# A hybrid encoder layer on one core: weight halves copied ahead of mixed sums, identity turns between phases, and two late waits

## The reference, cut to what matters

```python
xn = rms_norm(h, g_attn_pre)
qa, ka, va, qb, kb, vb = split(xn @ w_in)
ya = mixer_a(...)        # 8 query heads, 2 key heads, softmax over all 2048 keys
yb = mixer_b(...)        # 8 heads, three dilated windows with a bias table
y = concat([rms_norm(ya, g_out_a), rms_norm(yb, g_out_b)]) @ w_out
h = h + rms_norm(y, g_attn_post)
f = square(relu(rms_norm(h, g_mlp_pre) @ w_ff1)) @ w_ff2
h = h + rms_norm(f, g_mlp_post)
h = h + sigmoid(rms_norm(h, g_ple) @ w_ple_gate) * (p @ w_ple_proj)
```

## Time and profile before

| | |
|---|---|
| three runs | 3360.53, 3360.77, 3361.61 us |
| profiled execution | 3360.36 us, span 3358.6 us |
| PE busy | 3294.1 us (98%) |
| DVE, ACT, POOL busy | 2278.8 (68%), 1853.5 (55%), 1851.7 us (55%) |
| mean granted PE clock | 0.996 |

### The profile page before, as it was taken

The page is one execution under the profiler, slowest core; times in us unless marked ns, Lnnn a source line. Parts: engine busy times, 40 slices in busy tenths (PEclk is TensorE's granted clock), DMA queues, the critical chain, the costliest instruction groups (busy, mean ns, idle before and its releaser), DMA issues.

```text
span 3358.6 us, 48304 instructions
## 1 busy us (share of the span) xinstructions
PE 3294.1 (98%) x17246; PEld 2767.0 (82%) x17246; DVE 2278.8 (68%) x4080; ACT 1853.5 (55%) x3576; POOL 1851.7 (55%) x1434
## 2 busy tenths in 40 slices
PE   8999999999999989998999999999999999999999
PEld 7888878888888879997888888888888888888887
DVE  6556579999999989997646565555746556565555
ACT  3221178888888879998434354344543435443333
POOL 5555534454452168883477732777407776057771
PEclk9999999999999999999999999999999999999999
DMA  5554433444442234344244456444474444744444
GB/s 192 165 185 152 142 104 139 154 169 157 157 143 75 62 88 104 95 99 173 78 138 151 151 194 251 144 154 147 163 250 163 147 155 144 262 155 143 143 149 158
DMA packets 223915, 503.39 MB, mean 150 GB/s; under 512 B 105428, under 2 KB 123420, under 8 KB 204476
## 3 DMA queue, kind: packets, MB, share of 16 engines
q1 hardware_dynamic: 214332, 486.57, 43.9%
q10 hardware_dynamic: 9344, 13.73, 1.1%
HBM read 417.09 MB, written 95.58 MB: 153 GB/s over the span
## 4 chain that ended last, share of the span: by engine, by line
PE 44%; DVE 4%; ACT 2%; POOL 2%; issue 1%; DMA 1%; SPq 0%; ACTq 0%; DVEq 0%
PE feed_bank L1906 41%; DVE feed_sums L2397 1%; PE feed_bank L1991 1%; PE feed_bank L1897 1%; POOL feed_v_hl L1863 1%; POOL feed_qT L1863 0%; PE feed_bank L2014 0%; DMA feed_y_in<-scr_yB 0%; DVE feed_xT L2321 0%; ACT feed_rl L2201 0%; ACT feed_rl L2203 0%; PE feed_bank L2046 0%; POOL feed_kT L1863 0%; ACT feed_v_hl L2186 0%; DVE feed_sums L2394 0%
## 5 line engine op out<-in xcount | busy, mean ns | idle before, releaser
L1863 POOL TENSOR_TENSOR feed_v_hl<-feed_w_raw,feed_v_hl 128x1024 fp32r<-128x1024 f32 x176 | 437.6, 2496 | 138.6 <-ACT feed_v_hl L2186 133.0
L1906 PE MATMUL feed_bank<-feed_v_hl,feed_comb 128*128 128x512 f32 x1776 | 416.5, 390 | 3.1 <-POOL feed_v_hl L1863 3.1
L1906 PEld LDWEIGHTS feed_bank<-feed_v_hl,feed_comb 128*128 128x128 f32 x1776 | 331.8, 188 | 74.5 <-POOL feed_v_hl L1863 6.3
L1126 DVE TENSOR_TENSOR mixa_pT<-mixa_turned,mixa_pT 128x512 fp32r<-128x512 f32 x512 | 350.9, 685 | 58.9 <-ACT mixa_pT L1068 52.5
L1068 ACT ACTIVATE mixa_pT<-mixa_turned 128x512 fp32r<-128x512 f32 x512 | 306.7, 599 | 118.7 <-PE mixa_turned L1004 99.6
L949 PE MATMUL mixa_out_acc<-mixa_pT,mixa_v_hl 128*128 128x512 f32 x1028 | 365.7, 437 | 0.2
L2413 DVE TENSOR_TENSOR feed_total<-feed_total,feed_bank 128x512 f32<-128x512 f32 x352 | 223.9, 682 | 190.2 <-PE feed_bank L1906 187.4
L2382 DVE TENSOR_TENSOR feed_comb<-feed_rl,feed_comb 128x256 fp32r<-128x256 f32 x128 | 138.9, 1085 | 312.1 <-ACT feed_comb L2205 311.7
L1906 PE MATMUL feed_bank<-feed_xT,feed_v_hl 128*128 128x512 f32 x1488 | 344.3, 390 | 3.1 <-ACT feed_rl L2201 3.1
L2201 ACT ACTIVATE feed_rl<-feed_bank 128x512 f32<-128x512 f32 x128 | 76.4, 597 | 490.2 <-PE feed_bank L1906 483.5
L1906 PEld LDWEIGHTS feed_bank<-feed_xT,feed_v_hl 128*128 128x128 f32 x1488 | 280.2, 188 | 62.0 <-issue 3.7
(11 more groups left out here) (263 smaller groups left out, 7099.6 us busy)
## 6 DMA issues: line engine op xcount, KB each, us to landing
feed_w_raw<-scr_wT SPq DMA_DIRECT2D x160, 512.0 KB, 3.3
feed_w_raw<-w_tail_dram SPq DMA_DIRECT2D x128, 512.0 KB, 3.5
proj_w_raw<-w_in_dram SPq DMA_DIRECT2D x36, 1024.0 KB, 5.3
feed_v_hl<-scr_wG SPq DMA_DIRECT2D x34, 1024.0 KB, 5.1
feed_w_raw<-w_ff_dram SPq DMA_DIRECT2D x64, 512.0 KB, 3.4
feed_qT<-scr_wG SPq DMA_DIRECT2D x17, 1024.0 KB, 4.8
feed_kT<-scr_wG SPq DMA_DIRECT2D x17, 1024.0 KB, 5.1
scr_table<-scr_bias SPq DMA_DIRECT2D x8, 1520.0 KB, 9.0
```

The costliest lines, as they stand in the source:

```text
L1126: ve.tensor_tensor(pT[1][:, s % NR, :], turned[s % 2][:], pT[0][:, s % NR, :].bitcast(F32), ALU.subtract).then_inc(lo_done, 1)
L1863: pool.tensor_tensor(w_sp[slot][:, 1, :], w_raw[:, slot, :], w_sp[slot][:, 0, :].bitcast(F32), ALU.subtract).then_inc(w_lo, 1)
L1906: mm = pe.matmul(dst, lhs, rhs, start=start, stop=stop)
```

## The change

Three things change.

1. ACT's list in the feed: at chunk (m, g, 0, 0) it takes two upper weight halves, `weight_hi(i + 3)` as before and `weight_hi(i + 4)`, and only then `mixed_hi(g, 3)`; at the next chunk it takes none.
2. PE turns the identity, with no reader, at five places: 14 times at the end of the projection, 36 times at the start of mixer B behind the four that are there, 16 times at the end of mixer B, 32 times at the start of the feed and 24 times behind the first turn of data there.
3. SP no longer waits for the last store of each row tile at the end of the projection: SP waits in mixer A in front of the load of mixer B's v, and ACT in front of its first turned tile. At the end of mixer B SP waits only for the stores of the first buffer; the last store is awaited in the feed behind the first raw weight loads. For that `st_out`, `y_st` and a semaphore `y_last` move to objects that outlive the phase.

```diff
@@ FeedInputs, FirstInputs
+        self.y_st = k.sb("y_st", [P, 2, 4, HD], side="right")
+        self.y_last = k.sem("y_last")
+        self.st_out = k.sems("st_out", TT)
@@ project_phase, SP and PE
             for s in st_out:
-                sp.wait_ge(s, 16 * (4 * NBLK + 1))
+                sp.wait_ge(s, 16 * (4 * NBLK))
+            for _ in range(14):
+                pe.transpose(tp[0][:, 0:P], ident[:], ident[:])
@@ mixer_a_phase, SP before heads.load_v, ACT before the loop over tiles
+            for s in first.st_out:
+                sp.wait_ge(s, 16 * (4 * NBLK + 1))
+            for s in first.st_out:
+                act.wait_ge(s, 16 * (4 * NBLK + 1))
@@ mixer_b_phase, SP and PE
-            for s in y_out:
-                sp.wait_ge(s, 32 * NHB + 16)
+            sp.wait_ge(y_out[0], 32 * NHB + 16)
+            for _ in range(36):
+                pe.transpose(score[1][:, BANK:BANK + P], ident[:], ident[:])
+            for _ in range(16):
+                pe.transpose(score[0][:, 0:P], ident[:], ident[:])
@@ feed_phase, SP behind the raw loads, PE, ACT
+            sp.wait_ge(feed.y_last, 32 * NHB + 16)
+            keep_on(32)
             turn(0, 0)
+            keep_on(24)
                 for i, c in enumerate(FF):
-                    if i + 3 < NFF and FF[i + 3][0] == "m":
+                    if i + 3 < NFF and FF[i + 3][0] == "m" and FF[i - 1][2:] != (0, 0):
                         weight_hi(i + 3)
...
                     elif c[2:] == (0, 0):
+                        weight_hi(i + 4)
                         mixed_hi(c[1], 3)
```

More of the change, by code:

```diff
@@ L260, in project_phase @@
         qo_ready, ko_ready = k.sem("qo_ready"), k.sem("ko_ready")
-        st_out = k.sems("st_out", TT)
+        st_out = first.st_out
         qo_out, ko_out = k.sem("qo_out"), k.sem("ko_out")
@@ L1174, in mixer_b_phase @@
         y_part = k.sb("y_part", [P, 2, 2, P])
-        y_st = k.sb("y_st", [P, 2, 4, HD])
+        y_st = feed.y_st
         score = [ctx.enter_context(nc.psum_tensor(f"mixb_score{i}", [P, 2 * BANK], F32)) for i in range(2)]
@@ L1189, in mixer_b_phase @@
         rden_done, y_ready = k.sem("rden_done"), k.sem("y_ready")
-        y_out = k.sems("y_out", 2)
+        y_out = [k.sem("y_out"), feed.y_last]
         K_DMAS, Q_DMAS, V_DMAS = heads.K_DMAS, heads.Q_DMAS, heads.V_DMAS
@@ L1995, in first_out, with keep_on @@
                 mm.then_inc(acc_done, 1)
+            def keep_on(count):
+                for _ in range(count):
+                    pe.transpose(acc[3][:, 0:P], ident[:], ident[:])
+            keep_on(32)
             turn(0, 0)
+            keep_on(24)
             for t in range(TT):
```

## The result

| | before | changed |
|---|---|---|
| median of 11 runs each | 3360.80 us | 3369.82 us |
| lowest and highest | 3359.00, 3364.43 | 3368.59, 3373.65 |
| profiled execution, its span | 3360.36, 3358.6 us | 3369.76, 3368.0 us |

The ratio is 1.0026, with a 95% interval of 1.0018 to 1.0034: 9.0 us slower. The forecast was 3371.4 us, on the slower side.

What follows compares the result with a forecast made beforehand. The prediction took PE, busy for 98% of the span, as the bound. Its terms, 16.4 - 1.65 - 1.0 - 3.2 = +10.6 us, gave 3371.4 us on the median, range 3347 to 3378.

Steps and rivals of the forecast that it cites:

- The boundary: Feed, chunk (m, g, 2, 0): POOL's subtraction delays DVE's fifth sum 2.34 us, PE starts 1.26 later, thirteen times: +16.4 us.
- no obstacle: Rival at the feed boundary: DVE's fifth sum passes ahead of or beside POOL's subtraction, 13 x 0.36 saved; 3350.2 us, chance 0.20.
- either way: Rival at the feed boundary: the order of DVE's sum and POOL's subtraction swaps at about half the places; 3360.8 us, chance 0.14.
- Projection to A: Projection to mixer A: without SP's store wait the phase starts at 433.7, not 435.32: -1.65 us; clock 1.00 anyway.
- A to B: Mixer A to mixer B: 36 turns hold the clock, DVE's first bias addition comes 1.0 earlier, POOL's row then gates: -1.0 us.
- B to feed: Mixer B to feed: earlier start without the store wait -1.3, first turn -0.25, first 12 products at full clock -1.65: -3.2 us.
- cold-turns rival: Phase changes: turns don't hold the clock and stand in front of needed work; with the port effect 3386 us, chance 0.08.

Runs made afterwards that it cites:

- Experiment 1: Kernel before with only ACT's new weight order (upper half for chunk (m, g, 2, 0) copied ahead of the mixed sums): 3376.71 us, ratio 1.0044.
- experiment 3: Changed kernel, but POOL waits ahead of the lower half of chunk (m, g, 2, 0) until DVE's fifth mixed sum is done: 3356.14 us, ratio 0.9984.
- experiment 4: Kernel of experiment 3, with DVE also adding the first product's tile 0 results ahead of the mixed lower half: 3345.69 us, ratio 0.9956.
- experiment 5: Kernel before with the late store waits alone, without turns and with ACT's old weight order: 3356.70 us, ratio 0.9986.
- experiment 6: Kernel before with the turns alone, without late store waits and with ACT's old weight order: 3357.58 us, ratio 0.9988.
- experiment 2: Changed kernel with ACT's old weight order, so turns and late store waits alone: 3355.29 us, ratio 0.9982.
- experiment 8: Changed kernel with DVE adding the first product's tile 0 results ahead of the mixed lower half, POOL not held: 3352.90 us, ratio 0.9974.
- experiment 7: Kernel of experiment 6 without the 16 turns ending mixer B and with 72 instead of 32 starting the feed: one run, 3364.58 us.

## Why the prediction was right

**The boundary: right in mechanism and size.** Forecast was a fifth sum that ends 2.34 later and a PE start 1.26 later, thirteen times, 16.4. Against the start of PE's twelve products the fifth sum now ends 2.20 later. Those products take 4.47 from start to start (2218.08 to 2222.55) for 3.25 before, 1.22 more; the sum of the trace is 15.6. The mean is 1.20 for 1.26. Experiment 1 shows that the order causes it, experiment 3 that of the order the overlap does. One reading was loose: of the five sums from 1660.2 to 1670.3 only the three beside a subtraction of POOL take 2.6 us; two take 1.25 beside POOL copies of 1.2. One sum per POOL operation holds. The port rivals (no obstacle, either way) are out: the wait of 1.6 stands at all 13 places. The Trainium skill, "SBUF — State Buffer", "Who interferes with whom", says that a DVE instruction with two SBUF inputs contends with a GpSimd instruction that reads SBUF, and that whichever issues first has the ports to itself to the end. The rows agree: 2.61 behind POOL, 0.41 ahead of it. The same section of the Trainium skill says that with one SBUF input there is no contention; DVE's additions, whose other input is a PSUM bank, take 0.64 each beside POOL's two subtractions in experiment 4.

**Projection to A: -2.04 for -1.65.** About 1.5 of it is the step; 0.5 is luck, since PE's last product ended at 431.31 in this execution and at 431.83 before, and nothing ahead of it was changed. Phase A's start came 0.45 behind PE's last turn. The 14 turns do stand in front: experiment 5 has none, and phase A starts 1.61 behind PE's last product there, 1.97 here. The step's other statement, that the clock is at 1.00 there anyway, rested on one execution: in experiment 1, where nothing in this phase was changed, the same 24 turns behind the same 3.48 us ran at 0.50.

**A to B: mis-sized, -0.26 for -1.0.** The clock held and the first bias addition came 0.74 sooner behind the phase's first turn, but PE's first turn of the probabilities then waited 1.34 for POOL, and by the last product of B 0.26 was left. That POOL's row gates PE was in the step; how much of the 1.0 it eats was not. Even the 0.26 isn't shown to be the turns' work: from B's first turn to its last product the three traces without turns take 381.03 to 381.98 us, the eight with them 380.54 to 381.70.

**B to feed: -3.12 for -3.2.** From B's last product to the second tile's turn: -1.31 by the wait, the rest by the clock. The two hang together: without the turns the wait's part was lost again (experiment 5, -0.05), the turns alone gave -1.84 (experiment 6), and where the clock fell as the 16 turns began both gave only -1.93 (experiment 2).

**The end: 0.7 unforeseen.** From the last boundary to the last products the changed kernel gained 10.09 - 9.40: a wait of PE for DVE's norm at 3294.07, 0.93 before, is 0.23 now. The same obstacle is at work. In the chain to that norm DVE subtracts two SBUF operands while POOL subtracts weights, and this row is 0.71 shorter, because it begins 0.90 us into POOL's instruction (3291.08) and no longer about 0.2:

```profile
3281.90 3.29 DVE L2447 TENSOR_TENSOR feed_comb<-feed_y_in,feed_comb 128x1024 fp32r<-128x1024 f32 x1 [1.04 <-ACT feed_comb L2225]
...
3291.98 2.58 DVE L2468 TENSOR_TENSOR feed_comb<-feed_y_in,feed_comb 128x1024 fp32r<-128x1024 f32 x1 [1.04 <-ACT feed_comb L2246]
```

In experiments 2, 3, 4 and 8 the row takes 3.31, 2.58, 2.67 and 3.20, and PE's wait is 0.95, 0.22, 0.32 and 0.84: always 2.35 or 2.36 less.

Sum of the profile: 15.6 - 2.04 - 0.09 - 0.26 - 3.12 - 0.7 = +9.4, as measured, where -0.09 is what phase A itself gained. The forecast sum was +10.6. The terms missed by -0.8, -0.5, +0.7, +0.1 and -0.7; that they cancel in part is luck. The cold-turns rival falls by the rows at 1.00 and by experiment 7; where turns did run at 1.2 GHz (experiment 2), it cost 1.2 us in the feed, and the clock was at 1.00 again before the first turn of data. In the rival "no obstacle" the price was too small: its 13 x 0.36 is 8.6, by experiment 4.

## What to carry to other kernels

Before a copy is moved forward, follow the instruction that it releases on another engine: where that one holds up a third engine's critical instruction, order the two by a wait, shorter one first (0.41 us ahead or 2.61 behind). Where an engine stands idle for another's result, put work that is ready into that time (two additions of 1.27 us into an idle time of 1.34). Price a repeated wait in front of a pipelined engine by start-to-start times, not by its idle row.

## What was not expected of the hardware

A stop in front of PE costs more than its idle row: 0.66 us for a row of 0.37 (experiments 2 and 4). Of the other 0.29, 0.16 is overlap that the stop forfeits: when PE runs through, the next row starts 0.16 before the one ahead of it ends (2211.22 + 2.88 = 2214.10, against 2213.94). The last 0.13 is that the 24 products behind a stop take 5.57 from start to start and not 5.44; the rows don't show why.

Turns alone raise the granted clock from 0.50 to 1.00 (experiment 7). The Trainium skill, "TensorE: Matmul & The Clock Gate", Part 4, says that the full rate doesn't engage for them; the measurement decides against it here.

The clock behind one and the same gap differs between executions. At the projection's end it was 1.00 in the earlier trace rows, 0.50 in experiment 1 after an equal gap; in experiment 6 it was 0.66 from 435 to 440. Behind the feed's first stall of 3.1 us the same 24 products take 5.56 us from start to start in experiment 5, 7.1 to 7.2 in the kernels before and changed, 8.3 in experiment 4. Leads are therefore read within one trace, from one landmark to the next.
